# Matrix products of a four-layer kernel: order of the high and low terms, grouped 512-column runs, and the first gate piece by token blocks

## The chip, the cores and the metric

One core of a Trainium2 chip runs the whole program. The metric is the device time of one execution in microseconds, as the median of three runs of the kernel before: 895.15 us (894.41 to 895.58). The engines are named as in the profile: PE (matrix products), PEld (its weight loads), DVE (vector), ACT (scalar), POOL (GpSimd) and SP (it issues most of the DMAs).

## The reference

256 tokens of width 1024 in fp32 go through two blocks. The first has two layers, each a mixer and a feed-forward part; the second has one layer.

```python
# layer 0: x = x + ab_mixer(rms_norm(x));  layer 1: x = x + mla_mixer(rms_norm(x), positions)
# after each: hf = rms_norm(x); x = x + square(relu(hf @ ffn_w1)) @ ffn_w2        (1024 -> 4096 -> 1024)
# then x = rms_norm(x, final_norm), and the second block:
h = rms_norm_2(x, g_pre_mix);  m = chunk_relpos_attention(h, w_qkv, w_o, rel_bias)
x = x + rms_norm_2(m, g_post_mix)
h = rms_norm_2(x, g_pre_ffn)
x = x + rms_norm_2((silu(h @ w_gate) * (h @ w_up)) @ w_down, g_post_ffn)          (1024 -> 2816 -> 1024)
```

The mla_mixer projects x to a small latent (`c_w_in`, 672 columns), that to queries (`c_w_uq`) and to keys and values (`c_w_ukv`), rotates a part of both, and attends in 16 heads.

## The kernel before, in words

**Split products.** Every fp32 matrix product is made of three products in fp32r: each operand is cut into a high part and a low part, and hi·hi + hi·lo + lo·hi is summed in PSUM. Weights come in pieces of 128 x 2048 (1 MB, one DMA each on SP's queue) into a ring of three slots `raw`. ACT copies a piece to `w_hi` (`hi`, L755, or in quarters L764), then DVE writes `w_lo = raw - w_hi` (`lo`, L1231, quarters L1238). PE waits for both (`split`). ACT may start the high copy of piece n when PE has used piece n-3 (`piece_used`); SP loads piece n when the low part of piece n-3 is written. Activations are turned by PE (transposes into PSUM banks 4 to 7), then ACT copies them to `h_hi` (L784), and DVE writes `h_lo` (L1256); both lie in `h_both`. PE waits for `h_lo` (`h_wait`). Each engine works through its list strictly in the written order; nothing but that and semaphores sets the order.

**Feed-forward parts.** `ffn` works in 16 chunks of 256 hidden columns. The first piece is multiplied in `stationary_seam`, beside the transposes of the late part of x (`turn_late`). From the second on, `stationary_both` makes a chunk's hidden values: for each half of 128 columns and each of eight blocks k one product of `w_hi` (stationary) with `h_both`, 512 columns wide (high and low side by side, L1963), followed by one of `w_lo` with `h_hi`, 256 wide (L1965). DVE adds the two halves (`TENSOR_REDUCE`, L1540), squares the positive part, ACT and DVE split it into `g_hi` and `g_lo`, and `out_piece` multiplies it with the second weight, all products 512 columns wide. PE makes hidden chunk c+1 before it multiplies out chunk c. In the first of these parts DVE also builds two small tables after chunk 0 (`tables`, L1498 to L1518, at `between()`).

**The seams.** Before each `ffn`, before the latent projection and before the second block the last product is followed at once by residual additions on DVE, transposes on PE, `h_hi` on ACT and `h_lo` on DVE: `seam`, `out_seam`, `turn`. The first consumers are `stationary_seam`, `latent_in` and `moving_slice`.

**The latent part.** POOL turns the sums of squares into scales (`rms`), at its end two `q_scale` (L697). ACT then writes the queries (`q_out`, L1010), a weight piece's high copy, a rotated key (L1017) and the high part of the turned key-value latent (`turn_latent_kv`, L995), whose low part is DVE's L1594. PE's key products wait for that low part. In the attention loop `c_fill` puts pieces of the output projection between the heads from step 9 on.

**The gated part.** 11 chunks, each a gate piece, an up piece and a down piece. The first gate piece is multiplied once all 256 tokens are turned (`turn_glu(0)`, ten warming products `warm`, `turn_glu(1)`), with the weights stationary; the first up piece (`gate_up(0)`) is made of 256-column products, and in its midst `spread_row` makes the row of scales that ACT copies (`row_out`, L810) and DVE multiplies into the gate (`glu_first`, L1812). Then ACT takes the silu, DVE multiplies with the up values (`mul_plain`, L1819; in the middle chunks `glu_mul`, a reduce L1833 and a product L1836). PE's up piece of chunk c+1 waits for this product of chunk c (`mul_out`). At the end `out_last_two` waits once for the last chunk's `g_lo`.

## Time and profile before

| what | value |
|---|---|
| median of three runs | 895.15 us |
| the profiled execution | 894.42 us, span 892.6 us |
| PE busy | 877.9 us, 98% of the span |
| DVE, ACT, POOL busy | 617.4, 441.2, 80.2 us |
| mean granted PE clock | 0.999 |
| HBM traffic | 173 GB/s over the span |

The span runs from the first to the last instruction of the profiled execution; what remains to its own time, 1.8 us, lies around it. Matmuls are pipelined: a row's duration holds the way through the array, so the pace of PE is read from the starts of consecutive rows, not from their durations. "Busy" therefore also counts small stalls as work.

### The profile page before, as it was taken

The page shows a single profiled execution, that of the slowest core. Times are in us where ns is not written, and L with a number is a line of the kernel's source. Part 1 is how long each engine was busy: PE and PEld are TensorE (multiplying, and loading weights), DVE is VectorE, ACT ScalarE, POOL GpSimd, SP SyncE. Part 2 cuts the span into 40 slices and gives each one's busy share as a digit, 9 for nine tenths or more (in the row PEclk, how much of TensorE's full clock was granted, in tenths as well). Part 3 has the DMA queues.
Part 4 walks back from the last instruction along what each step waited for, and adds up shares of the span by engine and source line. Part 5 has one row for each costly group of instructions (what it writes and reads, how often), then busy time and mean ns, then how long its engine had stood idle before and what let it go on. Part 6 is the DMA issues. An engine that isn't in the chain of part 4 may idle for free.

```text
span 892.6 us, 12512 instructions
## 1 busy us (share of the span) xinstructions
PE 877.9 (98%) x4898; PEld 748.0 (84%) x4898; DVE 617.4 (69%) x781; ACT 441.2 (49%) x586; POOL 80.2 (9%) x114
## 2 busy tenths in 40 slices
PE   9999999999999999999999999999999999999997
PEld 8988888888888877778888888879987888888886
DVE  6999777666666668857666666665775676676674
ACT  5795544433333577745333333374555644434432
POOL 3663110000000030011000000010000200000000
PEclk9999999999999999999999999999999999999999
DMA  9764445655554361375555555537333446555541
GB/s 296 246 211 151 147 148 200 213 190 189 188 188 170 108 206 54 100 252 196 200 190 190 191 190 197 189 125 240 131 135 95 142 144 233 189 185 191 188 142 48
DMA packets 97818, 155.87 MB, mean 175 GB/s; under 512 B 4079, under 2 KB 72332, under 8 KB 97772
## 3 DMA queue, kind: packets, MB, share of 16 engines
q1 hardware_dynamic: 95068, 149.37, 49.7%
q0 software_dynamic: 1648, 5.80, 2.1%
q8 instruction: 31, 0.51, 0.2%
q10 hardware_dynamic: 1056, 0.07, 0.1%
q14 instruction: 15, 0.12, 0.0%
HBM read 153.62 MB, written 1.09 MB: 173 GB/s over the span
## 4 chain that ended last, share of the span: by engine, by line
PE 87%; DVE 6%; ACT 3%; SPq 1%; issue 1%; POOL 1%; DMA 1%; DVEq 0%; POOLq 0%; ACTq 0%
PE psum L1963 20%; PE psum L1882 17%; PE psum L1884 16%; PE psum L1883 16%; PE psum L1965 10%; DVE w_lo L1231 2%; PE psum L2370 1%; ACT w_hi L755 1%; DVE h_both L1256 1%; PE psum L2400 1%; ACT h_both L784 1%; PE psum L2476 1%; SPq L517 1%; PE psum L2383 1%; PE psum L1903 1%
## 5 line engine op out<-in xcount | busy, mean ns | idle before, releaser
L1231 DVE TENSOR_TENSOR w_lo<-raw,w_hi 128x2048 fp32r<-128x2048 f32 (+3 forms) x116 | 260.3, 2251 | 93.8 <-ACT w_hi L755 50.0
L1963 PE MATMUL psum<-h_both,w_hi 128*128 128x512 f32 x784 | 278.5, 398 | 0.0
L1965 PE MATMUL psum<-h_both,w_lo 128*128 128x256 f32 x784 | 220.0, 281 | 0.0
L1963 PEld LDWEIGHTS psum<-h_both,w_hi 128*128 128x128 f32 x784 | 147.3, 188 | 36.3 <-DVE w_lo L1231 0.3
L1965 PEld LDWEIGHTS psum<-h_both,w_lo 128*128 128x128 f32 x784 | 148.0, 189 | 1.4
L755 ACT ACTIVATE w_hi<-raw 128x2048 fp32r<-128x2048 f32 (+2 forms) x71 | 129.6, 1837 | 35.6 <-PE psum L1884 33.9
L1882 PE MATMUL psum<-w_hi,g_hi 128*128 128x512 f32 x368 | 145.0, 394 | 0.7 <-DVE g_lo L1840 0.4
L1883 PE MATMUL psum<-w_lo,g_hi 128*128 128x512 f32 x368 | 143.6, 390 | 0.0
L1884 PE MATMUL psum<-w_hi,g_lo 128*128 128x512 f32 x368 | 143.5, 390 | 0.0
L773 ACT ACTIVATE w_hi<-raw 128x2048 fp32r<-128x2048 f32 x66 | 125.9, 1910 | 24.9 <-PE psum L1884 24.9
L940 ACT ACTIVATE g_hi<-g_mul 128x512 fp32r<-128x512 f32 x32 | 20.2, 633 | 171.0 <-DVE g_mul L1544 171.0
L1882 PE MATMUL psum<-w_hi,h_both 128*128 128x512 f32 (+1 forms) x226 | 90.6, 401 | 2.1 <-ACT arena L1033 0.9
L1884 PE MATMUL psum<-w_hi,h_both 128*128 128x512 f32 (+1 forms) x226 | 86.1, 381 | 0.0
L1883 PE MATMUL psum<-w_lo,h_both 128*128 128x512 f32 (+1 forms) x226 | 85.8, 380 | 0.0
L1882 PEld LDWEIGHTS psum<-w_hi,g_hi 128*128 128x128 f32 x368 | 69.1, 188 | 16.5 <-issue 1.3
L1882 PE MATMUL psum<-h_both,w_hi 128*128 128x256 f32 x272 | 78.8, 290 | 3.1 <-DVE h_both L1594 1.2
L1884 PEld LDWEIGHTS psum<-w_hi,g_lo 128*128 128x128 f32 x368 | 69.1, 188 | 15.0
L1883 PEld LDWEIGHTS psum<-w_lo,g_hi 128*128 128x128 f32 x368 | 69.1, 188 | 12.6
L629 POOL TENSOR_SCALAR msq<-ssq 128x1 f32<-128x1 f32 (+1 forms) x22 | 15.7, 715 | 709.5 <-ACT junk L799 682.2
L1883 PE MATMUL psum<-h_both,w_hi 128*128 128x256 f32 x272 | 76.9, 283 | 0.0
L1884 PE MATMUL psum<-h_both,w_lo 128*128 128x256 f32 x272 | 76.9, 283 | 0.0
L1540 DVE TENSOR_REDUCE g_act<-psum 128x512 f32<-128x1024 f32 x30 | 36.7, 1224 | 36.2 <-PE psum L1965 36.2
(275 smaller groups left out, 1082.5 us busy)
## 6 DMA issues: line engine op xcount, KB each, us to landing
raw<-in_ffn_w SPq DMA_DIRECT2D x64, 1024.0 KB, 5.3
raw<-in_w_qkv SPq DMA_DIRECT2D x12, 1024.0 KB, 5.2
raw<-in_ab_w_in SPq DMA_DIRECT2D x11, 1024.0 KB, 6.2
raw<-in_w_gate SPq DMA_DIRECT2D x11, 1024.0 KB, 5.4
raw<-in_w_up SPq DMA_DIRECT2D x11, 1024.0 KB, 5.4
raw<-in_w_down SPq DMA_DIRECT2D x11, 1024.0 KB, 5.6
raw<-in_ab_w_out SPq DMA_DIRECT2D x4, 1024.0 KB, 4.9
raw<-in_c_w_out SPq DMA_DIRECT2D x4, 1024.0 KB, 5.7
```

The lines of the kernel that those rows point to most:

```text
L517: return engine.dma_start(vecs[r0:r0 + v.shape[0], :], v)
L629: step(pool.tensor_scalar(msq[:, c0:c0 + n], ssq[:, c0:c0 + n], 1.0 / w, EPS, ALU.mult, ALU.add))
L755: ins = act.activation(dst, src, ACT.Copy)
L773: act.activation(w_hi[:, slot, :], raw[:, slot, :], ACT.Copy).then_inc(hi_ready, 1)
L940: act.activation(g_hi[:, r, :], g_mul[:, r, :], ACT.Copy).then_inc(g_hi_ready, 1)
L1231: ins = dve.tensor_tensor(dst, src, high, ALU.subtract)
L1540: ins = dve.tensor_reduce(g_act[:, r, :].rearrange("p (f t) -> p f t", f=2), sums_of(hidden_banks(c)), AX.X, ALU.add)
L1882: pe.matmul(dst, stat[0], mov[0], start=first, stop=False, skip_group_check=shared)
L1883: pe.matmul(dst, stat[0], mov[1], start=False, stop=False, skip_group_check=shared)
L1884: return pe.matmul(dst, stat[1], mov[0], start=False, stop=last, skip_group_check=shared)
L1963: pe.matmul(bank(b + f), wh[:, k, cs], h_both[:, k, :, :].rearrange("p u s -> p (u s)"), start=k == 0, stop=False, skip_group_check=True)
L1965: ins = pe.matmul(bank(b + f)[:, 0:S], wl[:, k, cs], h_hi[:, k, :], start=False, stop=k == KB - 1, skip_group_check=True)
```

## The change

- `stationary_both` issues the eight 512-column products of a half first, then its eight 256-column ones.
- At the first use of turned activations (`stationary_seam`, and in the same way `latent_in` for token block 0 and `moving_slice`) PE waits for the high part only, issues the two products that need it (`w_hi` and `w_lo` with `h_hi`, or the like), then waits for the low part and issues the third. `stationary_seam` writes bank 0 instead of bank 4.
- The first gate piece is computed with the tokens stationary, per block of 128 tokens, block 0 before `turn_glu(1)`; the warming products are gone. ACT copies the result to SBUF (`gate_out`), PE turns it with four transposes inside the first up piece. The first and the last up piece now use the 512/256 form, so DVE's product of chunk 0 has a reduce ahead of it.
- The last chunk's hidden values are made in two halves of 256 (`mul_block`, `lo_block`), and `out_last_two` waits for each.
- On ACT the high copy `hi(P_UQ + RING)` stands ahead of `q_out(0)`; on POOL the `rms` jobs and `q_scale` are interleaved by token block, and glu0 comes ahead of pm1; `qf_wait(7)` moves from step 9 of the attention to step 11; DVE's two tables come after chunks 2 and 3.

```diff
             pool.wait_ge(rel_built, 1)
             pool.dma_start(rel_dram.ap(), rel_ext[:, :]).then_inc(rel_stored, 16)
-            for name in ("c0", "c1", "ckv0", "cq0", "ckv1", "cq1"):
+            for name in ("c0", "c1"):
                 rms(name)
             for tb in range(TB):
+                rms(f"ckv{tb}")
+                rms(f"cq{tb}")
                 cq, c = JOBS[f"cq{tb}"][0], JOBS[f"c{tb}"][0]
                 pool.wait_ge(rstd_ready, JOB_AT[f"cq{tb}"] + 1)
                 pool.tensor_scalar(q_scale[:, tb:tb + 1], rstd[:, cq:cq + 1], float(C_QK) ** -0.5, rstd[:, c:c + 1],
 
             rms("pm0")
+            rms("glu0")
             rms_halves("pm1", 0)
-            rms("glu0")
             rms("glu1")
             rms("pf0")
                                          scale=q_scale[:, tb:tb + 1])
                 ins.then_inc(evac_q, 1)
 
+            hi(P_UQ + RING)
             q_out(0)
-            hi(P_UQ + RING)
             act.wait_ge(krr_turned, 1)
             act.activation(krT[C_NOPE:C_QK, :], psum[C_NOPE:C_QK, 4, 0:S], ACT.Copy).then_inc(krT_ready, 1)
             turn_latent_kv()
...
+            def squares_glu(tb):
+
+                act.wait_ge(x_ready, X_AT["glu"] + 2 * tb + 2)
+                squares(x[:, tb, :], JOBS[f"glu{tb}"][0])
+
+            def gate_out(tb):
+
+                if tb == 0:
+                    act.wait_ge(gate_made, 1)
+                else:
+                    act.wait_ge(piece_used, P_GLU + 1)
+                act.activation(g_mul[:, 2, tb * CH:(tb + 1) * CH], bank(tb)[:, 0:CH], ACT.Copy).then_inc(gate_copied, 1)
+
             squares_0(4, "pm0", 1.0)
             hi(P_GLU)
+            squares_glu(0)
             squares_1(4, P_O2 + 3, "pm1", 1.0, 0, 0)
             turn_glu(0)
             squares_1(4, P_O2 + 3, "pm1", 1.0, 0, 1)
             hi(P_GLU + 1)
+            gate_out(0)
             turn_glu(1)
-            squares_x(("glu0", "glu1"), X_AT["glu"])
+            squares_glu(1)
+            gate_out(1)
             hi(P_GLU + RING - 1)
             row_out(2, 2)
...
+                if isinstance(c, int) and c == GC - 2:
+                    for f in range(2):
+                        cs = slice(f * S, (f + 1) * S)
+                        act.wait_ge(mul_out, hb + GC + f)
+                        act.activation(g_hi[:, (j + 1) % 2, cs], g_mul[:, (j + 1) % 2, cs], ACT.Copy)\
+                            .then_inc(g_hi_ready, 1)
+                    return
...
                 hidden(0, first)
                 lo(first + RING)
-                if between:
-                    between()
                 for c in range(1, FC):
                         lo(n + 1 + RING)
+                    if between and c in (2, 3):
+                        between[c - 2]()
...
 
             def glu_first():
 
-                dve.wait_ge(piece_used, first + 1)
-                dve.tensor_tensor(in_blocks(g_act[:, 0, :]), in_blocks(bank(0)),
+                dve.wait_ge(gate_turned, 1)
+                dve.tensor_tensor(in_blocks(g_act[:, 0, :]), in_blocks(bank(3)),
                                   r_row[:, :].unsqueeze(1).to_broadcast([P, 2, S]), ALU.mult).then_inc(gate_scaled, 1)
 
-            def mul_plain(c, n_up):
-
-                dve.wait_ge(act_out, c + 1)
-                dve.wait_ge(piece_used, n_up + 1)
-                dve.tensor_tensor(g_mul[:, c % 2, :], g_act[:, c % 2, :], bank(6), ALU.mult).then_inc(mul_out, 1)
+            def mul_block(r, f, n_up):
+
+                if f == 0:
+                    dve.wait_ge(up_half, 1)
+                else:
+                    dve.wait_ge(piece_used, n_up + 1)
+                cs = slice(f * S, (f + 1) * S)
+                dve.tensor_reduce(g_mul[:, r, cs], sums_of(6)[:, f], AX.X, ALU.add).then_inc(up_in, 1)
+                dve.wait_ge(up_in, GC + f)
+                if f == 0:
+                    dve.wait_ge(act_out, GC)
+                dve.tensor_tensor(g_mul[:, r, cs], g_act[:, r, cs], g_mul[:, r, cs], ALU.mult).then_inc(mul_out, 1)
-            mul_plain(0, first + 1)
+            glu_mul(0, 0, first + 1)
             glu_lo(0, 0)
...
+                    mul_block(r, 0, n + 1 + 6 * i)
+                    lo_block(r, 0)
+                    mul_block(r, 1, n + 1 + 6 * i)
+                    lo_block(r, 1)
+                    return
...
+                    for k in range(KB):
                         ins = pe.matmul(bank(b + f)[:, 0:S], wl[:, k, cs], h_hi[:, k, :],
                                         start=False, stop=k == KB - 1, skip_group_check=True)
+                    if f == 0 and half_done is not None:
+                        ins.then_inc(half_done, 1)
...
+                    h_hi_wait(t, 2 * q)
+                    for f in range(2):
+                        for k in (2 * q, 2 * q + 1):
+                            at = bank(b)[:, f * S:(f + 1) * S]
+                            pe.matmul(at, wh[:, k, f * P:(f + 1) * P], h_hi[:, k, :], start=k == 0 and f == 0,
+                                      stop=False, skip_group_check=True)
+                            pe.matmul(at, wl[:, k, f * P:(f + 1) * P], h_hi[:, k, :], start=False, stop=False,
+                                      skip_group_check=True)
                     h_wait(t, 2 * q)
                     for f in range(2):
                         for k in (2 * q, 2 * q + 1):
-                            ins = product(bank(b)[:, f * S:(f + 1) * S],
-                                          (wh[:, k, f * P:(f + 1) * P], wl[:, k, f * P:(f + 1) * P]),
-                                          h_block(k), k == 0 and f == 0, k == KB - 1, True)
+                            ins = pe.matmul(bank(b)[:, f * S:(f + 1) * S], wh[:, k, f * P:(f + 1) * P], h_lo[:, k, :],
+                                            start=False, stop=k == KB - 1, skip_group_check=True)
                     if q == 0:
                         turn_late(x_at)
                 ins.then_inc(piece_used, 1)
...
+                for k in range(2):
+                    ready(k)
+                    wh = w_hi[:, n_slot, :].rearrange("p (k c) -> p k c", k=2)
+                    wl = w_lo[:, n_slot, :].rearrange("p (k c) -> p k c", k=2)
+                    for h in range(2):
+                        cs = slice(h * 512, (h + 1) * 512)
+                        ins = product(bank(h), act_of(k, 0), (wh[:, k, cs], wl[:, k, cs]), False, k == 1)
+                ins.then_inc(acc_part, 1)
...
                 if i == 9:
                     qf_wait(6)
+                if i == 11:
                     qf_wait(7)
...
-            warm(10, 1)
+            def gate_tokens(tb):
+
+                wh = w_hi[:, P_GLU % RING, :].rearrange("p (k c) -> p k c", k=KB)
+                wl = w_lo[:, P_GLU % RING, :].rearrange("p (k c) -> p k c", k=KB)
+                for k in range(KB):
+                    if k % 2 == 0:
+                        pe.wait_ge(h_hi_ready, t_base(T_GLU) + tb * KB // 2 + k // 2 + 1)
+                    high_terms(bank(tb)[:, 0:CH], h_block(k, tb), (wh[:, k, :], wl[:, k, :]), k == 0)
+                for k in range(KB):
+                    if k % 2 == 0:
+                        pe.wait_ge(h_lo_ready, t_base(T_GLU) + tb * KB // 2 + k // 2 + 1)
+                    ins = low_term(bank(tb)[:, 0:CH], h_block(k, tb), (wh[:, k, :], wl[:, k, :]), k == KB - 1)
+                return ins
+
+            split(P_GLU)
+            gate_tokens(0).then_inc(gate_made, 1)
             turn_glu(1)
-            split(P_GLU)
-            wh = w_hi[:, P_GLU % RING, :].rearrange("p (k c) -> p k c", k=KB)
-            wl = w_lo[:, P_GLU % RING, :].rearrange("p (k c) -> p k c", k=KB)
-            for q in range(KB // 2):
-                pe.wait_ge(h_lo_ready, t_base(T_GLU) + KB // 2 + q + 1)
+            gate_tokens(1).then_inc(piece_used, 1)
+
+            def up_first():
+
+                n = P_GLU + 1
+                wh = w_hi[:, n % RING, :].rearrange("p (k c) -> p k c", k=KB)
+                wl = w_lo[:, n % RING, :].rearrange("p (k c) -> p k c", k=KB)
+                pe.wait_ge(hi_ready, n + 1)
                 for f in range(2):
-                    for k in (2 * q, 2 * q + 1):
-                        ins = product(bank(0)[:, f * S:(f + 1) * S],
-                                      (wh[:, k, f * P:(f + 1) * P], wl[:, k, f * P:(f + 1) * P]),
-                                      h_block(k), k == 0 and f == 0, k == KB - 1, True)
-            ins.then_inc(piece_used, 1)
+                    for k in range(KB):
+                        pe.matmul(bank(6 + f), wh[:, k, f * P:(f + 1) * P],
+                                  h_both[:, k, :, :].rearrange("p u s -> p (u s)"),
+                                  start=k == 0, stop=False, skip_group_check=True)
+                    if f == 0:
+                        for tb in range(TB):
+                            pe.wait_ge(gate_copied, tb + 1)
+                            for g in range(2):
+                                ins = pe.transpose(bank(3)[:, g * S + tb * P:g * S + (tb + 1) * P],
+                                                   g_mul[:, 2, tb * CH + g * P:tb * CH + (g + 1) * P], ident[:, :])
+                        ins.then_inc(gate_turned, 1)
+                split(n)
+                for f in range(2):
+                    for k in range(KB):
+                        ins = pe.matmul(bank(6 + f)[:, 0:S], wl[:, k, f * P:(f + 1) * P], h_hi[:, k, :],
+                                        start=False, stop=k == KB - 1, skip_group_check=True)
+                    if f == 0:
+                        spread_row(2, 2)
+                ins.then_inc(piece_used, 1)
+
             hb, first = 2 * FC, P_GLU
 
             def gate_up(c, r, n0, i):
                 split(n0 + 6 * i)
-                pe.wait_ge(gate_scaled, c)
+                if not (isinstance(c, int) and c == 1):
+                    pe.wait_ge(gate_scaled, c)
                 stationary_both(n0 % RING, 4)
                 split(n0 + 1 + 6 * i)
                 pe.wait_ge(mul_out, hb + c)
-                if isinstance(c, int) and c == GC - 1:
-                    stationary((n0 + 1) % RING, T_GLU, 6)
-                else:
-                    stationary_both((n0 + 1) % RING, 6)
+                stationary_both((n0 + 1) % RING, 6, up_half if isinstance(c, int) and c == GC - 1 else None)
...
```

How the order changes at three places. First PE, in a feed-forward part: the end of the first weight piece and the second one (L1963 and L1965 before are L2024 and L2027 now). Before:

```order
L1884 MATMUL psum<-h_both,w_lo 128x256
L1963 MATMUL psum<-h_both,w_hi 128x512
L1965 MATMUL psum<-h_both,w_lo 128x256
L1963 MATMUL psum<-h_both,w_hi 128x512
L1965 MATMUL psum<-h_both,w_lo 128x256
L1963 MATMUL psum<-h_both,w_hi 128x512
```

and now:

```order
L2050 MATMUL psum<-h_both,w_hi 128x256 x4
L2024 MATMUL psum<-h_both,w_hi 128x512 x8
L2027 MATMUL psum<-h_both,w_lo 128x256 x8
L2024 MATMUL psum<-h_both,w_hi 128x512 x8
L2027 MATMUL psum<-h_both,w_lo 128x256 x8
L1930 MATMUL psum<-w_hi,g_hi 128x512
```

Sixteen alternations became four runs of eight; the number of products is the same.

Second ACT, in the latent part: the query output (q_scale), a weight piece's high copy in two views, the rotated key and the turned latent. Before:

```order
L755 ACTIVATE w_hi<-raw 128x1536
L1010 ACTIVATE arena<-psum,q_scale 128x512 x2
L755 ACTIVATE w_hi<-raw 128x2x512 x2
L1017 ACTIVATE arena<-psum 32x256
L995 ACTIVATE h_both<-psum,cols 128x256 x2
```

and now:

```order
L761 ACTIVATE w_hi<-raw 128x1536
L761 ACTIVATE w_hi<-raw 128x2x512 x2
L1016 ACTIVATE arena<-psum,q_scale 128x512 x2
L1023 ACTIVATE arena<-psum 32x256
L1001 ACTIVATE h_both<-psum,cols 128x256 x2
```

The two copies moved ahead of the query output; what follows is as before.

Third DVE, at the start of the gated part: scaled gate, low part of a weight piece, product with the up values, low part of it, and the next chunk. Before:

```order
L1812 TENSOR_TENSOR g_act<-psum,r_row 128x512
L1231 TENSOR_TENSOR w_lo<-raw,w_hi 128x2048
L1819 TENSOR_TENSOR g_mul<-g_act,psum 128x512
L1840 TENSOR_TENSOR g_lo<-g_mul,g_hi 128x512
L1231 TENSOR_TENSOR w_lo<-raw,w_hi 128x2048
L1825 TENSOR_REDUCE g_act<-psum 128x512
```

and now:

```order
L1843 TENSOR_TENSOR g_act<-psum,r_row 128x512
L1260 TENSOR_TENSOR w_lo<-raw,w_hi 128x2048
L1878 TENSOR_REDUCE g_mul<-psum 128x512
L1881 TENSOR_TENSOR g_mul<-g_act,g_mul 128x512
L1885 TENSOR_TENSOR g_lo<-g_mul,g_hi 128x512
L1260 TENSOR_TENSOR w_lo<-raw,w_hi 128x2048
L1870 TENSOR_REDUCE g_act<-psum 128x512
```

One reduce is added between the weight piece and the product.

## Rows read from the trace of the kernel before

**Rows 1.** The page: busy time of each engine.
```profile
PE 877.9 (98%) x4898; PEld 748.0 (84%) x4898; DVE 617.4 (69%) x781; ACT 441.2 (49%) x586; POOL 80.2 (9%) x114
```
**Rows 2.** Timeline of PE, first feed-forward part: start us, us, engine, line, operation.
```profile
202.56 0.39 PE L1963 MATMUL psum<-h_both,w_hi 128*128 128x512 f32 x1
202.78 0.28 PE L1965 MATMUL psum<-h_both,w_lo 128*128 128x256 f32 x1
202.90 0.40 PE L1963 MATMUL psum<-h_both,w_hi 128*128 128x512 f32 x1
...
206.08 0.40 PE L1963 MATMUL psum<-h_both,w_hi 128*128 128x512 f32 x1
```
**Rows 3.** Timeline of PE, the products just before, all of 512 columns.
```profile
199.84 0.39 PE L1882 MATMUL psum<-w_hi,g_hi 128*128 128x512 f32 x1
...
202.33 0.39 PE L1884 MATMUL psum<-w_hi,g_lo 128*128 128x512 f32 x1
```
**Rows 4.** Timeline of PE, query and key projection, all of 256 columns.
```profile
640.38 0.28 PE L1884 MATMUL psum<-h_both,w_lo 128*128 128x256 f32 x1
...
642.89 0.28 PE L1884 MATMUL psum<-h_both,w_lo 128*128 128x256 f32 x1
```
**Rows 5.** Timeline of PE, seam ahead of the first feed-forward part ([idle before <-releaser]).
```profile
116.35 0.40 PE L1884 MATMUL psum<-w_hi,h_both 128*128 128x512 f32 x1
117.07 0.36 PE L1882 MATMUL psum<-h_both,w_hi 128*128 128x256 f32 x1 [0.33 <-DVE h_both L1256]
...
121.23 0.38 PE L1882 MATMUL psum<-h_both,w_hi 128*128 128x256 f32 x1 [0.19 <-DVE h_both L1256]
```
**Rows 6.** Timeline of ACT, the same seam.
```profile
115.18 0.84 ACT L784 ACTIVATE h_both<-psum,cols 128x256 fp32r<-128x256 f32 x2 [2.81 <-PE psum L1903]
```
**Rows 7.** Waits of PE: us in total, times, longest us.
```profile
PE psum L1882 <- DVE h_both L1256: 1.7, 6, 0.3
```
**Rows 8.** Timeline of PE, first feed-forward part, out piece of chunk 1.
```profile
140.88 0.28 PE L1965 MATMUL psum<-h_both,w_lo 128*128 128x256 f32 x1
141.45 0.50 PE L1882 MATMUL psum<-w_hi,g_hi 128*128 128x512 f32 x1 [0.30 <-DVE w_lo L1231]
```
**Rows 9.** Timeline of DVE, the tables and hidden chunk 1.
```profile
131.16 0.17 DVE L1498 COPY rel_ext<-rel_t 16x64 f32<-16x64 f32 x1
...
134.66 1.22 DVE L1540 TENSOR_REDUCE g_act<-psum 128x512 f32<-128x1024 f32 x1
```
**Rows 10.** Timeline of PE, latent part: last query product, first key product, query transposes.
```profile
328.57 0.39 PE L1884 MATMUL psum<-w_hi,h_both 128*128 128x512 f32 x1
330.21 0.38 PE L1882 MATMUL psum<-h_both,w_hi 128*128 128x256 f32 x1 [1.25 <-DVE h_both L1594]
...
338.68 0.28 PE L1884 MATMUL psum<-h_both,w_lo 128*128 128x256 f32 x1
339.30 0.29 PE L2330 MATMUL psum<-ident,arena 128*96 128x128 f32 x1 [0.34 <-DVE arena L1648]
```
**Rows 11.** Timeline of ACT, latent part.
```profile
323.81 1.27 ACT L1010 ACTIVATE arena<-psum,q_scale 128x512 f32<-128x512 f32 x2 [3.85 <-POOL q_scale L697]
324.97 2.00 ACT L755 ACTIVATE w_hi<-raw 128x1024 fp32r<-128x1024 f32 x2
```
**Rows 12.** Timeline of POOL, latent part.
```profile
321.42 2.30 POOL L697 TENSOR_SCALAR q_scale<-rstd 128x1 f32<-128x1 f32 x2
```
**Rows 13.** Timeline of PE, attention step 9.
```profile
362.76 0.47 PE L1882 MATMUL psum<-w_hi,h_both 128*128 128x512 f32 x1 [0.90 <-ACT arena L1033]
```
**Rows 14.** Timeline of PE, start of the gated part, to its third up piece.
```profile
695.59 2.39 PE L2072 MATMUL psum<-ones 128*128 128x128 f32 x20
...
709.06 0.61 PE L2065 MATMUL psum<-diag,ones 128*128 128x128 f32 x4
...
734.94 0.50 PE L1963 MATMUL psum<-h_both,w_hi 128*128 128x512 f32 x1
```
**Rows 15.** Timeline of PE, the last chunk's out piece.
```profile
878.33 0.47 PE L1882 MATMUL psum<-w_hi,g_hi 128*128 128x512 f32 x1 [0.41 <-DVE g_lo L1840]
```

More of the change, by code:

```diff
@@ L1991, in moving_slice @@
                 tb = i // 2
+                ks = (2 * (i % 2), 2 * (i % 2) + 1)
                 if t is not None and tb == 0:
[L1993 to L1996 removed]
+                    h_hi_wait(t, 4 * j + ks[0])
+                    for k in ks:
+                        high_terms(bank(banks[tb]), h_block(4 * j + k, tb), (wh[:, k, :], wl[:, k, :]),
+                                   j == 0 and k == 0)
+                    h_wait(t, 4 * j + ks[0])
+                    for k in ks:
+                        ins = low_term(bank(banks[tb]), h_block(4 * j + k, tb), (wh[:, k, :], wl[:, k, :]),
+                                       j == 1 and k == 3)
+                else:
+                    for k in ks:
+                        ins = product(bank(banks[tb]), h_block(4 * (j if half is None else half) + k, tb),
+                                      (wh[:, k, :], wl[:, k, :]), j == 0 and k == 0, j == 1 and k == 3)
                 if i == 3:
```

77 lines of the change are left out of this document (46 added, 31 removed).

## The prediction, as it was made before the changed kernel had run

> **What bounds the kernel now.** I read the page first: PE is busy for 98% of the span [rows 1], so a change pays only where PE's own list gets shorter or where one of its few waits goes. The page's pipelined matmul durations hide small stalls, so next I read the timeline of PE by the starts of its rows, and then its waits. Six waits for the low part of turned activations (DVE L1256) add up to 1.7 us [rows 7]; four of them are the first product behind a seam and two a later one in the feed-forward seams. Each costs more than the idle time shown, since a matmul's modelled end lies past the point where the next could start. Lastly I read ACT, DVE and POOL around the few larger waits: tables, latent part, attention step 9, start and end of the gated part. The reader is to see that PE is fed everywhere else.
>
> **Grouping.** An alternating pair takes (206.08 - 202.90)/9 = 0.353 us [rows 2]. Products of 512 columns alone start every (202.33 - 199.84)/11 = 0.2264 us [rows 3], those of 256 alone every (642.89 - 640.38)/21 = 0.1195 us [rows 4], together 0.346. The first 512 of a piece, which follows another 512, is over after 0.22 (202.56 to 202.78 [rows 2]); in the mean the 512 that follows a 256 takes 0.353 - 0.118 = 0.235. So the extra 0.009 hangs on the 512 behind a 256, and a run of eight pays it once at most. Per half-piece: alternating 8 x 0.353 = 2.826 (first half 2.813, as its first pair takes 0.34); grouped 8 x 0.346 = 2.767, plus 0.009 in the second half. The saving is 0.046 to 0.050. The 784 pairs are 98 half-pieces; six lie in the gated part ahead of a wait that swallows them (below), so 92 x 0.048 = 4.4 us. Bounds: nothing, if the 0.009 belongs to the pair; 98 x 0.050 = 4.9.
> The Trainium skill (TensorE: Matmul & The Clock Gate, "Back-to-back issue gap") gives the distance of warm matmuls as columns/2.4 + 2.5 ns, whatever came before; by it the order of the widths is free and this term is 0. The rows are longer (0.226 and 0.120 against 0.216 and 0.109) and depend on the neighbour, so the trace does not agree; what is left of the rule is the first rival.
>
> **High part first.** PE is through with the piece ahead of the first feed-forward seam at 116.35 + 0.23 = 116.58, but starts at 117.07 [rows 5]; ACT's high part is there at 115.18 + 0.84 = 116.02 [rows 6]. So the 0.49 goes, and 0.08 of slow restart (the first product takes 0.20 to the next instead of 0.12). The eight high terms (0.96 us) cover DVE's low part, which released PE before. PE's later transposes come 0.5 earlier too, the second pair of high parts with them, and the second wait goes: 0.19 idle [rows 5] and 0.28 - 0.12 = 0.16 of modelled overlap make 0.35, plus 0.1 restart. That is 1.0 us per feed-forward seam, twice: 2.0. Ahead of the latent projection and of the second block the first wait is of the same kind [rows 7], 0.49 each, 1.0 together; there the next piece's last quarter of w_lo, behind DVE's turned blocks, still ends last, so no second gain.
>
> **Tables.** DVE does the tables from 131.16 to 134.66 and so reaches hidden chunk 1 late [rows 9]; its low part of the next weight piece then releases PE at 141.45, where 141.00 would do [rows 8]: 0.45. Without the tables chunk 1 comes some 3.4 us earlier. At their new places they stand before chunks whose results PE wants a whole hidden and out piece later (two pieces of some 5.6 us less about 4 of DVE and ACT), so I cost them at nothing; without that cover it would be the 3.5 us again.
>
> **Latent part.** PE waits from 328.57 + 0.23 to 330.21 for the low latent: 1.41 [rows 10]. Ahead of it on ACT: 3.85 idle until POOL's q_scale, query output 1.27, weight copy 2.00 [rows 11, 12]. With the copy first, it fits into that idle time (its slot is free when PE ends the first query piece, near 319.8), and POOL's second q_scale, which with the first took 2.30, is one short instruction. ACT then reaches the turned latent about 3.6 us earlier, DVE's low part is ready near 327, and PE goes on at 328.8. The next wait, 339.30 instead of 338.80 [rows 10], is for DVE's copy behind the rotation of the queries; that starts behind the last query output and a low part, both over 2 us earlier: 0.5 more. Together 1.9. Bounds: 0, if another release of PE takes over at once, and 1.9, as there is no more idle time.
>
> **Step 9.** PE waits 0.90 for ACT's L1033 (`qf_wait(7)`) [rows 13], with overlap and restart 1.0. Only bank 0 is written in steps 9 and 10, so the wait can stand at step 11. Next would be the transposes of head 7; DVE has normalised it near 361.8, PE reaches them at 362.5. Gain 1.0, bounds 0 and 1.1.
>
> **Start of the gated part.** PE's own list: ten warming products and the waits go, 4 transposes (0.44) come, two half-size up runs become 16 x 0.227 + 16 x 0.12 instead of 48 x 0.12. Laid out from 695.59 [rows 14]: token block 0 to 698.6, transposes as before to 699.6 (they wait for x), block 1 at ACT's pace of 0.5 per pair to about 702.8 (its product ended at 706.2 before), up piece to 709.2 instead of 712.4: 3.2 us ahead. But what PE needs next hangs on the scale row: spread (709.06 [rows 14]), ACT copy, gate product, table load, silu, weight copy, DVE low part, product, and so on without a break to the low part that releases PE at 734.94 [rows 14]. The spread comes at about 707.9, 1.1 earlier; the added reduce (1.22 for this shape [rows 9]) is longer by 0.1 than that. PE's next up piece waits for this product (`mul_out`), a new stall of about 2 us near 714.8, and up piece 2 starts at about 735.1. So the 3.2 is handed back, with the grouping of three pieces: term +0.1. Bounds: +0.5 and -3.2.
>
> **End.** Before, PE waits for g_lo until 878.33 [rows 15]. Now a half needs reduce 0.6, product 0.36, copy 0.4, subtraction 0.36, each engine waiting for the other; first half ready at about the same time, the second 1.8 later. PE has 1.4 of work between them, and the last up piece is shorter by 0.2: in all 0.3 lost; bounds 0.6 lost and 0.5 won.
>
> **Sum.** 4.4 + 2.0 + 1.0 + 0.45 + 1.9 + 1.0 - 0.1 - 0.3 = 10.3 us. From the profiled 894.42 that leaves 884.1; the median of the runs lies 0.73 above the profiled one, so 884.8.
>
> **Rivals.**
> First, the 0.009 belongs to the pair, not to the order: 884.8 + 4.4 = 889.2. For it: one pair only shows the short 512, at 0.01 us resolution. Against: the paces of rows 3 and 4. Chance 0.09.
> Second, the waits in the latent part and at step 9 are replaced by others: DVE's rotation or the heads' max and exp end last, 884.8 + 2.9 = 887.7. For it: ACT, DVE and POOL form one chain there. Against: each link shifts by more than the stall. Chance 0.12.
> Third, PE isn't held by the scale-row chain, the gated part keeps its 3.2: 881.5. For it: the stall at 734.94 before is small. Against: all links stand close. Chance 0.05.
> Fourth, slower: a run of 512-column products that reads h_both and reloads weights each time is slower than alternation. No row shows such a run. All else is worth 5.9 us, so it decides from (5.9 + 1.8)/784 = 0.010 us per pair, a pace of 0.243 in a run; at 0.25 the grouping costs 784 x 0.0165 = 12.9 instead of winning 4.4, and the time is 902. Against: the runs of rows 3, same width and as many weight loads. Chance 0.02.
> The grouping not being done at all is excluded by the order of instructions.
>
> **Numbers.** Forecast 0.70 at 884.8; rivals 0.09, 0.12, 0.05, 0.02; 0.02 for several losses together, near 893. Range 882.5 to 889.3: it reaches to the first two rivals and takes in the bounds of the grouping, and leaves the third and fourth out. A median of this kernel tells 0.2% (1.8 us) from no change. Faster by more 0.95, within 0.02, slower 0.03.
>
> **What would show it.** Grouped: L2024 starts 0.227 apart, L2027 0.120, a piece 5.54 instead of 5.65. Seams: no wait of 0.3 for h_both. Tables: no idle before the out piece of chunk 1. Latent part: no 1.25 us gap ahead of the keys, the keys' first product under 1 us behind the last query product. Gated part: an idle PE of about 2 us ahead of the second up piece, its releaser DVE's g_mul, and the third up piece as late after the seam as before. End: two waits of 0.4 to 0.6 for g_lo. Wrong it would be if L2024 keeps 0.235, or if new waits of over 1 us stand elsewhere.

## The result: 885.25 us, 9.9 us faster

The changed kernel takes 885.25 us (median of four runs, 884.83 to 885.42) against 895.12 us (894.41 to 895.58): a ratio of 0.989, with an interval of 0.9873 to 0.9907. The forecast was 884.8 us. The profiled execution took 885.36 us, span 883.6.

The two traces can be laid beside each other piece by piece: a weight piece ends in both with a product that releases the slot, so the start of that product is a marker, 141 of them in each trace. In the table an offset is the time of a marker in the changed kernel less its time before (negative: the changed kernel is ahead); the gain of a stretch is how far the offset falls over it.

| stretch (its markers' starts before, us) | offset at its ends | gain | forecast |
|---|---|---|---|
| start of the program (to 116.35) | 0 to +0.85 | -0.85 | none |
| seam, first feed-forward part (116.35 to 124.08) | +0.85 to -0.16 | 1.01 | 1.0 |
| tables (in the next 22.7 us) | | 0.57 | 0.45 |
| grouping, first part, 15 pieces (to 291.18) | -0.16 to -1.94, with the tables | 1.21 | 1.44 |
| seam, latent projection (297.56 to 304.65) | -1.94 to -2.51 | 0.57 | 0.49 |
| latent part (328.57 to 342.72) | -2.56 to -4.57 | 2.01 | 1.9 |
| attention, step 9 (342.72 to 388.92) | -4.57 to -5.64 | 1.07 | 1.0 |
| seam, second feed-forward part (400.73 to 408.46) | -5.64 to -6.64 | 1.00 | 1.0 |
| grouping, second part, 15 pieces (to 575.00) | -6.64 to -7.86 | 1.22 | 1.44 |
| seam, second block (581.38 to 588.32) | -7.86 to -8.47 | 0.61 | 0.49 |
| start of the gated part (695.36 to the third up piece, 734.94) | -8.46 to -8.26 | -0.20 | -0.1 |
| grouping, gated part, 16 pieces (734.94 to 869.14) | -8.26 to -9.67 | 1.41 | 1.54 |
| end (869.14 to 884.99) | -9.67 to -9.05 | -0.62 | -0.3 |

Without the first row the gains make 9.9 us, as the medians do (895.12 - 885.25 = 9.87). The 0.85 of the first row lies ahead of all that was changed. Over the traces of this study, whose programs are the same up to there, the first marker starts anywhere from 14.54 to 15.82 us. So one profiled execution against another is uncertain by that much. Stretches that no edit touches still differ by up to 0.2 us ahead of the marker at 85 us, and behind it they agree between two traces to some 0.05 us, most to 0.01. The profiled execution of `no_group` below took 1073.19 us at a mean granted clock of 0.753, against 888.41 to 889.33 us for its five others, and is left out, so that this run alone has no markers to lay beside the rest.

The page of the changed kernel, to compare with [rows 1]:

```profile
PE 872.0 (99%) x4850; PEld 748.4 (85%) x4850; DVE 620.3 (70%) x786; ACT 442.1 (50%) x589; POOL 79.1 (9%) x114
```

Its waits of PE (engine, line waited for, us in total, times, longest):

```profile
PE psum L2024 <- DVE g_mul L1881: 2.0, 1, 2.0
PE psum L2158 <- POOL ones L616: 1.0, 1, 1.0
PE psum L1930 <- DVE g_lo L1863: 0.9, 2, 0.6
PE psum L1989 <- DVE w_lo L1267: 0.5, 2, 0.3
```

The waits for turned activations [rows 7] are gone. New is the one for `g_mul`, and there are two for `g_lo` where one stood. The timeline of PE over one grouped piece, which answers to [rows 2]:

```profile
190.22 1.98 PE L2024 MATMUL psum<-h_both,w_hi 128*128 128x512 f32 x8
192.04 1.11 PE L2027 MATMUL psum<-h_both,w_lo 128*128 128x256 f32 x8
192.99 2.00 PE L2024 MATMUL psum<-h_both,w_hi 128*128 128x512 f32 x8
194.83 1.12 PE L2027 MATMUL psum<-h_both,w_lo 128*128 128x256 f32 x8
195.78 0.40 PE L1930 MATMUL psum<-w_hi,g_hi 128*128 128x512 f32 x1
```

By the starts, the runs take 1.82, 0.95, 1.84 and 0.95: 5.56 us. The run of 512 columns is 0.02 longer where it follows a 256; the prediction had 0.009, and the rows are read at 0.01. The first products behind the waits of [rows 8] and [rows 10] now follow at once:

```profile
140.65 0.40 PE L1930 MATMUL psum<-w_hi,g_hi 128*128 128x512 f32 x1
...
326.01 0.39 PE L1932 MATMUL psum<-w_hi,h_both 128*128 128x512 f32 x1
326.24 0.28 PE L1930 MATMUL psum<-h_both,w_hi 128*128 128x256 f32 x1
...
334.61 0.28 PE L1932 MATMUL psum<-h_both,w_lo 128*128 128x256 f32 x1
334.73 0.49 PE L2429 MATMUL psum<-ident,arena 128*96 128x128 f32 x3
```

Second up piece of the gated part, and the third, which answers to the last row of [rows 14]:

```profile
708.44 2.84 PE L2024 MATMUL psum<-h_both,w_hi 128*128 128x512 f32 x8 [1.97 <-DVE g_mul L1881]
711.08 0.63 PE L2027 MATMUL psum<-h_both,w_lo 128*128 128x256 f32 x2
...
726.68 1.55 PE L2024 MATMUL psum<-h_both,w_hi 128*128 128x512 f32 x6
```

The stall stands where it was forecast: PE idles from 706.47, which with the offset of 8.46 is 714.93 on the clock of the kernel before, against "near 714.8". But the run behind it takes 711.08 - 708.44 = 2.64 us instead of 1.82. The windows around it show why (length in us, then the busy time of PE, PEld, DVE, ACT and POOL, the granted clock, the DMA share, GB/s):

```profile
706.40:708.40 2.00, 0.07 (x1) 0.00 (x0) 1.86 (x3) 0.07 (x1) 0.00 (x0) 1.00 0.26 37
708.40:710.00 1.60, 1.56 (x6) 1.32 (x7) 0.69 (x1) 1.60 (x2) 0.00 (x0) 0.85 1.06 374
710.00:712.00 2.00, 2.00 (x8) 1.71 (x8) 1.21 (x1) 0.76 (x1) 0.00 (x0) 0.50 0.55 188
712.00:714.00 2.00, 2.00 (x10) 1.79 (x10) 2.00 (x2) 0.00 (x0) 0.00 (x0) 0.77 0.03 8
```

The clock falls to 0.50, the 1.2 GHz level. That was in no term. From its first product to its last the piece takes 715.54 - 708.44 = 7.10 us, against 5.57 in `mul_first` below at full clock (711.78 - 706.21). The Trainium skill (TensorE: Matmul & The Clock Gate, "HAM oscillation — how this bites in real kernels") says that PE falls back to half clock when it idles too long between products. The trace shows such a fall, but behind 1.97 us of idle time, a shorter gap than those the section warns of; the trace decides.

The end, which answers to [rows 15], has two waits where one stood:

```profile
868.65 0.47 PE L1930 MATMUL psum<-w_hi,g_hi 128*128 128x512 f32 x1 [0.57 <-DVE g_lo L1863]
...
870.63 0.47 PE L1930 MATMUL psum<-w_hi,g_hi 128*128 128x512 f32 x1 [0.36 <-DVE g_lo L1863]
```

### The profile page after: what moved, and what is told of

Same layout as the page of the kernel before. It is cut to its first block, busy times and chain, and to the rows that moved or that the text cites. A ratio compares the mean times of both kernels' runs of the same rounds, so it can differ in the third digit from the quotient of the medians.

```text
span 883.6 us, 12429 instructions
## 1 busy us (share of the span) xinstructions
PE 872.0 (99%) x4850; PEld 748.4 (85%) x4850; DVE 620.3 (70%) x786; ACT 442.1 (50%) x589; POOL 79.1 (9%) x114
## 4 chain that ended last, share of the span: by engine, by line
PE 92%; DVE 3%; ACT 1%; issue 1%; DVEq 0%; POOLq 0%; POOL 0%; ACTq 0%
PE psum L2024 20%; PE psum L1930 17%; PE psum L1931 16%; PE psum L1932 16%; PE psum L2027 10%; PE psum L2469 2%; PE psum L2499 1%; PE psum L1989 1%; PE psum L2576 1%; PE psum L2482 1%; PE psum L1951 1%; PE psum L1990 1%; PE psum L1994 1%; PE psum L2252 1%; PE psum L2587 1%
## 5 line engine op out<-in xcount | busy, mean ns | idle before, releaser
L2024 PE MATMUL psum<-h_both,w_hi 128*128 128x512 f32 x800 | 200.2, 392 | 2.0 <-DVE g_mul L1881 2.0
L2024 PEld LDWEIGHTS psum<-h_both,w_hi 128*128 128x128 f32 x800 | 146.7, 189 | 30.0 <-issue 2.1
L2027 PEld LDWEIGHTS psum<-h_both,w_lo 128*128 128x128 f32 x800 | 110.0, 192 | 7.9
L2027 PE MATMUL psum<-h_both,w_lo 128*128 128x256 f32 x800 | 112.3, 284 | 0.0
L1930 PE MATMUL psum<-w_hi,h_both 128*128 128x512 f32 (+1 forms) x202 | 82.1, 406 | 0.0
L1932 PE MATMUL psum<-w_hi,h_both 128*128 128x512 f32 (+1 forms) x202 | 77.9, 385 | 0.0
L1931 PE MATMUL psum<-w_lo,h_both 128*128 128x512 f32 (+1 forms) x202 | 77.7, 385 | 0.0
L1275 DVE TENSOR_TENSOR w_lo<-raw,w_hi 128x2048 fp32r<-128x2048 f32 x18 | 40.7, 2290 | 21.7 <-ACT w_hi L779 21.7
L1930 PE MATMUL psum<-h_both,w_hi 128*128 128x256 f32 x192 | 55.4, 289 | 0.3 <-DVE w_lo L1260 0.3
L1931 PE MATMUL psum<-h_both,w_hi 128*128 128x256 f32 x192 | 54.3, 283 | 0.0
```

Source lines behind the costliest of these rows:

```text
L1275: dve.tensor_tensor(w_lo[:, slot, :], raw[:, slot, :], w_hi[:, slot, :], ALU.subtract)\
L1930: pe.matmul(dst, stat[0], mov[0], start=first, stop=False, skip_group_check=shared)
L1931: pe.matmul(dst, stat[0], mov[1], start=False, stop=False, skip_group_check=shared)
L1932: return pe.matmul(dst, stat[1], mov[0], start=False, stop=last, skip_group_check=shared)
L2024: pe.matmul(bank(b + f), wh[:, k, cs], h_both[:, k, :, :].rearrange("p u s -> p (u s)"), start=k == 0, stop=False, skip_group_check=True)
L2027: ins = pe.matmul(bank(b + f)[:, 0:S], wl[:, k, cs], h_hi[:, k, :], start=False, stop=k == KB - 1, skip_group_check=True)
```

## Experiments

All times are medians, beside runs of the kernel before on the same chip (medians of 894.61 to 894.92 us); ratios are to it. The changed kernel was not run again beside them, and the executions of one kernel spread by 0.3 to 1.4 us. So differences of under 1 us from its 885.25 are read from the markers; the medians alone don't show them.

**Is it the order that saves the 0.009 us?** `group_only`, the kernel before and

```diff
                         pe.matmul(bank(b + f), wh[:, k, cs], h_both[:, k, :, :]...
+                    for k in range(KB):
                         ins = pe.matmul(bank(b + f)[:, 0:S], wl[:, k, cs], h_hi[:, k, :],
...
```

> The kernel before with one edit: in stationary_both the eight 512-column products of a half come first, then its eight 256-column ones; nothing else. My theory (the 512 behind a 256 takes 0.009 us more, and the order decides that): 0.08 to 0.09 us per hidden piece, 4.2 us in all, 890.9 us. First rival (the 0.009 belongs to the pair): 895.1. A third reading, that grouping pays only because other waits had gone as well: between the two, with new waits for w_lo in the trace.

890.99 us, ratio 0.9954 (0.994 to 0.9967). The first rival and the fourth fall: the order alone brings 3.9 us (3.53 by the markers, from the first seam on), and a run of 512 columns is not slow. By the markers each hidden piece of the feed-forward parts gains 0.09 and gives back 0.01 in the out piece behind it. What three pieces gain at the start of the gated part comes back at the third up piece, as forecast: 0.24 us, in a wait for the low part of the weights. Ahead of the first out piece behind the tables, 0.17 us go to the wait of [rows 8], which is now longer:

```profile
141.49 0.50 PE L1882 MATMUL psum<-w_hi,g_hi 128*128 128x512 f32 x1 [0.47 <-DVE w_lo L1231]
```

`no_group` is the changed kernel with that line taken out again.

> The changed kernel with the alternation of 512 and 256 columns put back in stationary_both. If the grouping is worth what the offsets between the two traces say (about 0.09 us per piece, 4.3 us together) this gives 889.4 us, some of it hidden in the wait for g_mul at the start of the gated part. If the gain of the changed kernel sits elsewhere: 885.3 to 887.

888.54 us, ratio 0.9926 (0.9912 to 0.9939): 3.3 us are lost, less than the 3.8 of the table and than the expected 889.4. Half a microsecond is within what executions scatter, and this run has no markers that could tell; the difference stays open. That the grouping saves some 3 to 4 us in both kernels is shown.

**Seams, and POOL's order.** `high_pool` is the kernel before with the edits of `stationary_seam`, `latent_in` and `moving_slice` (high part first), and on POOL the new order of the latent part

```diff
-            for name in ("c0", "c1", "ckv0", "cq0", "ckv1", "cq1"):
+            for name in ("c0", "c1"):
                 rms(name)
             for tb in range(TB):
+                rms(f"ckv{tb}")
+                rms(f"cq{tb}")
```

> The kernel before with the high part first at its four seams (bank 0 for the first feed-forward piece) and POOL's interleaved order of rms and q_scale; ACT's order as before. Theory: 1.0 at each feed-forward seam, 0.5 to 0.6 at each of the other two: 3.1 us. POOL's order gives ACT its scale 2.3 us earlier, which by itself would also cover the 1.41 us wait for the low latent: together 890.5 us. If only ACT's order counts there: 892.0. If the seams only shift the wait to the low part: 895.1 or 893.7.

889.99 us, ratio 0.9947 (0.9932 to 0.9962). By the markers it gains 1.01, 0.57, 1.00 and 0.61 at the four seams, and 1.51 + 0.47 at the two waits of the latent part. But 0.44 of the first seam's gain is given back four pieces later, at the same wait as above, now 0.74 us long:

```profile
140.76 0.50 PE L1884 MATMUL psum<-w_hi,g_hi 128*128 128x512 f32 x1 [0.74 <-DVE w_lo L1233]
```

So DVE, late by its tables, holds PE at a fixed time, and whatever PE wins ahead of them waits there. Moving them is worth the 0.57 of the table by itself (`order_act` below), and it also lets the first seam's gain through.

**ACT's order, step 9, tables.** `order_act`, the kernel before and

```diff
+            hi(P_UQ + RING)
             q_out(0)
-            hi(P_UQ + RING)
...
                 if i == 9:
                     qf_wait(6)
+                if i == 11:
                     qf_wait(7)
```

and the tables after chunks 2 and 3.

> The kernel before with three edits that lie apart and can be read apart in the trace: ACT's weight copy ahead of the query output (POOL's order stays), qf_wait(7) at step 11, the two tables after chunks 2 and 3. My theory: latent part between 1.4 and 1.9 us, step 9 1.0, tables 0.45, so 895.1 - 3.1 = 892.0 us. Rival two of the prediction (other releases take over): 894.6. If POOL's interleaved order is what the latent part needs, the 1.41 us wait for the low latent stays and the time is 893.6.

891.47 us, ratio 0.9961 (0.9946 to 0.9977). By the markers it gains 0.57 at the tables, 1.51 + 0.35 in the latent part and 1.07 at step 9. The second rival falls: no other release of PE takes over. And ACT's order and POOL's each remove the 1.41 us wait alone; together they are worth it once. The timeline of ACT here, then of POOL in `high_pool`:

```profile
323.94 1.27 ACT L1010 ACTIVATE arena<-psum,q_scale 128x512 f32<-128x512 f32 x2 [1.92 <-POOL q_scale L697]
325.23 0.38 ACT L1017 ACTIVATE arena<-psum 32x256 f32<-32x256 f32 x1
325.63 0.84 ACT L995 ACTIVATE h_both<-psum,cols 128x256 fp32r<-128x256 f32 x2
```

```profile
313.12 0.27 POOL L699 TENSOR_SCALAR q_scale<-rstd 128x1 f32<-128x1 f32 x1
...
320.17 0.31 POOL L699 TENSOR_SCALAR q_scale<-rstd 128x1 f32<-128x1 f32 x1
```

**The start of the gated part.** `old_start` is the changed kernel with the whole start as before (`mul_plain`, ten warming products, first gate piece with the weights stationary).

> The changed kernel with the start of the gated part as it was before (first gate piece with the weights stationary, ten warming products, first up piece in 256-column products, plain product on DVE); grouping, seams, latent part, step 9 and end as changed. My prediction's term: the new start is worth nothing, lost 0.1 us; the offsets of the two traces say it lost 0.35, so 884.9 us, and the granted clock of the profile back at 0.999. Third rival of the prediction (the new start keeps 3.2 us): 888.4.

885.27 us, ratio 0.989 (0.9875 to 0.9905): the same as the changed kernel. The third rival falls. By the markers `old_start`, against the changed kernel, is 3.47 us behind after the first gate piece, gains 0.29 in the first up piece (so the new start is 3.2 ahead there, as forecast) and 3.75 in the second, where it has no stall, and loses 0.46 at the third: 0.11 ahead in the end. The new start's win on PE is real and is handed back.

`mul_first` changes one place of the changed kernel, on DVE:

```diff
             glu_first()
+            glu_mul(0, 0, first + 1)
             lo(first + RING)
-            glu_mul(0, 0, first + 1)
```

> The changed kernel with one swap on DVE at the start of the gated part: the reduce and product of the first up piece (glu_mul) come ahead of the low part of the next weight piece instead of behind it. DVE was idle for 3.06 us before that low part, so reduce and product fit in there. Theory: PE's stall of 2.04 us ahead of the second up piece goes, and with it the lower granted clock behind it (0.8 us): 882.5 us. Rival (all links of the chain from the scale row to the low parts of the weights stand close, so another wait takes over within three pieces): 884.4 to 885.2.

881.66 us, ratio 0.985 (0.9836 to 0.9863), 3.6 us less; I had expected 2.8, with too little for the clock. The timelines of DVE, changed kernel and then `mul_first`:

```profile
700.39 0.69 DVE L1843 TENSOR_TENSOR g_act<-psum,r_row 128x512 f32<-128x512 f32 x1 [1.44 <-ACT r_row L816]
704.14 2.29 DVE L1260 TENSOR_TENSOR w_lo<-raw,w_hi 128x2048 fp32r<-128x2048 f32 x1 [3.06 <-ACT w_hi L761]
706.35 1.22 DVE L1878 TENSOR_REDUCE g_mul<-psum 128x512 f32<-128x1024 f32 x1
707.60 0.69 DVE L1881 TENSOR_TENSOR g_mul<-g_act,g_mul 128x512 f32<-128x512 f32 x1
```

```profile
700.73 1.22 DVE L1878 TENSOR_REDUCE g_mul<-psum 128x512 f32<-128x1024 f32 x1
702.13 0.69 DVE L1881 TENSOR_TENSOR g_mul<-g_act,g_mul 128x512 f32<-128x512 f32 x1 [0.19 <-ACT g_act L1202]
703.87 2.29 DVE L1260 TENSOR_TENSOR w_lo<-raw,w_hi 128x2048 fp32r<-128x2048 f32 x1 [1.04 <-ACT w_hi L761]
```

Reduce and product fill DVE's 3.06 us of idle time, and the low part starts when ACT's copy is there, as before. PE waits only some 0.16 us, for that low part, and goes on at full clock:

```profile
706.21 2.11 PE L2024 MATMUL psum<-h_both,w_hi 128*128 128x512 f32 x8
708.16 1.12 PE L2027 MATMUL psum<-h_both,w_lo 128*128 128x256 f32 x8
```

The markers show 3.48 us gained in this one piece (5.86 instead of 9.34) and nothing given back: 1.95 of waiting, 1.53 of clock. ACT's copies of the next weights move up with the product (`g_hi` at 703.74 instead of 708.33), and DVE's low parts ahead of the third up piece start at 719.99 instead of 724.11. That is more than PE gained, so the chain doesn't take it back.

`old_swap` is `old_start` with the same swap.

> The changed kernel with the old start of the gated part (885.27 us) and with DVE's product ahead of the low part of the weight, as in the fast version. If the 3.5 us came from the swap alone, 881.8. Theory: the swap only lets through what the new start had won on PE; in the old start PE is busy until the product is there anyway, so 885.0 to 885.3 us.

884.45 us, ratio 0.9885 (0.9868 to 0.9901). That is less than the expected 885.0. By the markers only one stretch behind the edit changes against `old_start`, by 0.46, at the third up piece. So the swap opens the way and the new start brings the rest; neither has much alone.

**The clock.** In the changed kernel warming products fill the stall, `warm(18, 1)`, then `warm(9, 1)` and `warm(4, 1)`, put ahead of `split(n0 + 1 + 6 * i)` for chunk 1.

> The changed kernel with 18 warming products of 128 columns (18 x 0.109 = 1.96 us) in the stall ahead of the second up piece, which stays. Theory: the granted clock fell to about half behind the stall because PE had been idle; with PE kept running it stays at 1.00 and the up piece takes 5.57 instead of 7.10 us: 885.25 - 1.5 = 883.7 us. Rival (the clock falls for another reason, the stall is all that counts): 885.2. If the next low part of a weight piece ends last instead, part of the 1.5 comes back as a wait for w_lo two pieces later.

885.45 us, ratio 0.9895 (0.988 to 0.991), granted clock 1.00 throughout. The expected 883.7 was missed, and the run settles little about the time: a call makes two rows, so the products ran from 706.11 to 710.05 and overran the stall. The up piece took 5.56 us, but began 1.8 later.

> The changed kernel with 9 warming calls in the stall ahead of the second up piece. The run with 18 showed that a call makes two rows of 0.109 us, so that 18 lasted 3.93 us and overran the stall; 9 last 1.96. Theory (an idle PE lets the granted clock fall behind it, at a cost of 7.10 - 5.57 = 1.5 us): the up piece starts at the same time as in the changed kernel and takes 5.56 us, 883.7 us in all. If PE is then held by a low part of a weight two pieces later, part of it comes back: up to 885.2.

884.66 us, ratio 0.9885 (0.9869 to 0.9902): most of the 1.5 us came back, the second case of the expectation. The up piece is 1.57 us shorter by the markers, and then 0.40 and 1.07 of it come back as waits for low parts of weights, at the next gate piece and at the third up piece. PE around them:

```profile
706.02 2.17 PE L2158 MATMUL psum<-ones 128*128 128x128 f32 x18
708.15 2.06 PE L2024 MATMUL psum<-h_both,w_hi 128*128 128x512 f32 x8
...
726.17 2.14 PE L2024 MATMUL psum<-h_both,w_hi 128*128 128x512 f32 x8 [0.79 <-DVE w_lo L1260]
```

This is the chain of the prediction: the third up piece starts 726.17 - 686.63 = 39.54 us after the last marker of the out projection; before the change it was 734.94 - 695.36 = 39.58, and in the changed kernel 726.68 - 686.90 = 39.78. The chain holds PE there, whether the clock falls or not. In the end the lower clock cost 0.2 us (39.78 against 39.54).

> The changed kernel with 4 warming calls (0.87 us) at the head of the same stall, so that PE then idles for some 1.1 us. The kernel before had a stall of 1.4 us ahead of the keys with the clock at 1.00 behind it, so I expect the same as with 9 calls, 883.7 us. If any idle time of PE here lets the clock fall, 885.2.

885.08 us, ratio 0.9887 (0.9871 to 0.9904). PE idles for 1.07 us behind the warming products, and the clock stays at 1.00:

```profile
706.64 1.06 PE L2158 MATMUL psum<-ones 128*128 128x128 f32 x8
708.77 2.08 PE L2024 MATMUL psum<-h_both,w_hi 128*128 128x512 f32 x8 [1.07 <-DVE g_mul L1881]
```

The 1.55 gained in the piece come back two and three markers later as 0.37 + 1.08, so the expected 883.7 was missed: the clock did stay up, but it was not worth the time.

**The end.** `old_end`, the changed kernel with the old end (`mul_plain`'s form, the last up piece in 256-column products, one `ready()`):

> The changed kernel with the old end (last up piece in 256-column products, one plain product and one wait for g_lo). The prediction's term was a loss of 0.3 us by the new end: 884.95. The offsets of the two traces say 0.6 to 0.8: 884.5. If the new end gains, 885.5 or more.

884.55 us, ratio 0.9882 (0.9866 to 0.9899): 0.7 us less; by the markers 0.60. Read from the markers, the new end as it stands is a loss. `both_first` is `mul_first` with the same idea at the end:

```diff
+                if isinstance(c, int) and c == GC - 2:
+                    mul_block(r, 0, n + 1 + 6 * i)
                 ahead(*a(0))
                 if isinstance(c, int) and c == GC - 2:
-                    mul_block(r, 0, n + 1 + 6 * i)
                     lo_block(r, 0)
```

> The version with reduce and product ahead of the low part at the start of the gated part (881.66 us), with the same swap at its end: the reduce and product of the first half of the last chunk come ahead of the low part of the last weight piece. Theory: the two stalls for g_lo at the end exist only because DVE sits idle for 2.5 us and then writes that low part first; both go: 0.73 + 0.52 + 0.17 for the slow restarts = 1.4, so 880.25 us. Rival (the end is bound by what follows the last products, or ACT's copies come too late): 881.2 to 881.7.

879.81 us, ratio 0.9835 (0.9822 to 0.9848): the fastest version, 5.4 us below the changed kernel. The markers give 1.44 us at the end, both waits for `g_lo` are gone. DVE in the changed kernel, then here:

```profile
864.24 2.29 DVE L1260 TENSOR_TENSOR w_lo<-raw,w_hi 128x2048 fp32r<-128x2048 f32 x1 [2.50 <-ACT w_hi L761]
866.45 0.68 DVE L1853 TENSOR_REDUCE g_mul<-psum 128x256 f32<-128x512 f32 x1
```

```profile
858.14 0.69 DVE L1853 TENSOR_REDUCE g_mul<-psum 128x256 f32<-128x512 f32 x1 [0.84 <-PE psum L2028]
858.87 0.42 DVE L1857 TENSOR_TENSOR g_mul<-g_act,g_mul 128x256 f32<-128x256 f32 x1
859.80 2.29 DVE L1260 TENSOR_TENSOR w_lo<-raw,w_hi 128x2048 fp32r<-128x2048 f32 x1 [0.51 <-ACT w_hi L761]
862.01 0.42 DVE L1863 TENSOR_TENSOR g_lo<-g_mul,g_hi 128x256 fp32r<-128x256 f32 x1
```

## Why the prediction was right, and where it was off

The sum was 10.3 us, the change is worth 9.9. The likeliest case came true, and none of the four rivals. Part of the closeness is luck: three terms were 1.0 us too high together (grouping 0.6, end 0.3, start 0.1), four 0.5 too low, and they partly cancel.

- **Grouping, 4.4 forecast, 3.84 measured.** Mechanism right, size off. The step that was mis-sized is "grouped 8 x 0.346 = 2.767". The pace of 512 columns, 0.2264, came from out products; in the grouped run it is 1.82/8 = 0.2275. And the 512 behind a piece's last 256 now starts 0.120 after it instead of 0.118. That makes 0.08 to 0.09 per piece instead of 0.096. The saving is a difference of numbers sixty times its size, read at 0.01 us. The prediction also sets the Trainium skill (TensorE: Matmul & The Clock Gate, "Back-to-back issue gap") against the rows: the section gives that formula as the isolated gap of a single matmul and says that in a stream with weight loads both operations set the distance, so the longer rows here don't speak against it as it is meant.
- **High part first, 3.0 forecast, 3.19 measured.** Both feed-forward seams came out to 0.01. The two others gave 0.57 and 0.61 instead of 0.49: the slow restart that I counted at the former was left out at the latter.
- **Tables, 0.45 and 0.57.** The same restart of 0.1 was left out. What I did not see is that this edit also protects the gains ahead of it; the sum was right because all edits were made together.
- **Latent part, 1.9 and 2.01.** Right in size. In the cause it is incomplete: I named ACT's copy and POOL's q_scale as one mechanism, and either is enough.
- **Step 9, 1.0 and 1.07.** Confirmed in `order_act`, apart from the rest.
- **Start of the gated part, -0.1 and -0.20.** The stall of "about 2 us" and its releaser were right, and so was "handed back". The chain came out as forecast: the spread row is made 1.27 us earlier (699.33 + 8.46 = 707.79 against 709.06), and the added reduce takes 1.25 of it back. The fall of the clock was missed. It costs 1.5 us in its piece, and 0.2 in the end, since the chain would have held PE anyway. What I did not see is that DVE idles for 3.06 us inside this chain, ahead of a low part; with reduce and product moved there (`mul_first`) the chain no longer holds PE, as the third rival had it.
- **End, -0.3 and -0.62.** The mis-sized steps are "the second 1.8 later" and the credit for "the last up piece is shorter by 0.2". "First half ready at about the same time" was right: PE starts on it 868.65 - 859.47 = 9.18 us after the last chunk's gate piece, 878.33 - 869.14 = 9.19 before. But the second half starts 1.98 later, not 1.8, since DVE's links are 0.68, 0.43 and 0.43 and ACT's copy 0.42 instead of 0.6, 0.36, 0.36 and 0.4. Six products cover 1.38 of that, so PE waits 0.52 and pays 0.08 for a second slow restart, 0.60 in all. And the up piece, shorter by 0.16, brings nothing, since the first wait takes it up (0.57 idle, 0.41 before). What I did not see is that both waits stand only because DVE writes the last weight's low part (2.29 us) ahead of the first half's reduce.

What I should have asked at both stalls is whether the instruction that PE waits for stands behind something that could come later. DVE was idle for 3.06 and 2.50 us just ahead; the place in the list, not the work, was the cost.

## What to carry to other kernels

When an edit gives PE time back and a stall appears behind it, look at the releaser's engine for idle time ahead of the releasing instruction: here two swaps on an engine that is 70% busy brought 4.9 us more by the markers, half as much again as the whole edit. Gains ahead of a wait whose release is fixed by another engine are lost until that wait is moved (here 0.44 of 1.01 us in `high_pool`, and the 3.2 of the new start), so the gains of single edits can't simply be added across it. Date edits by offsets between markers of two traces, not by whole runs.

## What the hardware did that I had not expected

- The granted clock of PE fell to 0.50 behind 1.97 us of idle time, and not behind 1.07 us; before the change it stayed at 1.00 behind 1.25 us of idle time [rows 10] (windows 328.80:330.20 and 330.20:334.00). `old_end`, with the same stall, shows the same fall: 0.50 from 709.52 to 712.90 in both traces. In `warm_9`, `mul_first` and `old_start`, where PE doesn't stall there for over 0.2 us, it doesn't fall. With other placement it might differ; only these cases were run.
- A POOL instruction of one column per partition takes 0.19 us, but 1.81 when it starts beside a low part on DVE (both operands of which, `raw` and `w_hi`, lie in SBUF). In the kernel before, POOL and then DVE:

```profile
317.97 1.81 POOL L629 TENSOR_SCALAR msq<-ssq 128x1 f32<-128x1 f32 x1 [3.69 <-ACT junk L799]
...
320.49 0.19 POOL L629 TENSOR_SCALAR msq<-ssq 128x1 f32<-128x1 f32 x1
```

```profile
317.99 1.75 DVE L1231 TENSOR_TENSOR w_lo<-raw,w_hi 128x1536 fp32r<-128x1536 f32 x1
```

It ends at 319.78, the low part at 319.74. The same holds for the 2.30 us of q_scale [rows 12], whose second instruction ends at 323.72, and DVE's low part of 321.92 + 1.75 = 323.67. The Trainium skill (SBUF — State Buffer, "Who interferes with whom") says that a DVE instruction with two SBUF inputs contends with a GpSimd instruction that reads SBUF, and calls the shared port pair an exclusive lock. The trace agrees: POOL's row ends 0.04 to 0.05 us after DVE's. This is what POOL's order changes: interleaved, only one q_scale is left to do at that place, and it ends at 320.17 + 0.31 = 320.48, before DVE's low part starts at 320.67.
